# Matmuls of 64 rows alternating between the partition halves in a two-layer attention and expert kernel, with the copies and waits around them moved

## The chip, the cores and the metric

The kernel runs on one core of a Trainium2 chip. The metric is the device time of one execution, in microseconds (us). All times are of the same program with the same inputs.

## The reference

256 tokens of width 1024 go through two layers. Each layer has a mixing part and an expert part:

```python
c_q, c_kv, k_r, n_q, n_kv, n_gate, m_gate = jnp.split(x @ w_in, offsets, axis=-1)
y_mla = mla_attention(q_nope, q_rope, k_nope, k_rope, v) @ w_branch_mla
y_nsa = nsa_attention(qn, kc, vc, k_sel, ..., k_win, ..., nsa_gates) @ w_branch_nsa
mixed = (g_mla * y_mla + g_nsa * y_nsa) @ w_out
x = layer_norm(DEEPNORM_ALPHA * x + mixed, ln1_g, ln1_b)
x = layer_norm(DEEPNORM_ALPHA * x + peer(x, ...), ln2_g, ln2_b)
```

`mla_attention` has eight heads with keys of 96 values (64 plus 32 rotary). `nsa_attention` has eight heads with keys of 64 values in two groups, and three branches: compressed keys (15 per group), selected blocks and a window; with 256 tokens the last two see every earlier token. `peer` scores 128 keys in each of two halves for eight heads (`s = einsum('thpd,hpnd->thpn', q, sub_keys)`, 64 values a half), takes the best 16 of each half and the best 16 of their 256 sums, and adds up those experts out of 128 x 128:

```python
a = jnp.einsum('chkd,cd->chk', expert_u[ec], xc)
w = gc * jax.nn.gelu(a, approximate=False)
y = jnp.einsum('chk,chkd->cd', w, expert_v[ec])
```

## The kernel before, in words

Weights come in tiles of 128 x 1024 through a ring of four slots (`raw`). SyncE loads a tile once TensorE has let go of its slot. ScalarE rounds it to `hi` (`split_hi`, L457), VectorE subtracts to get `lo` (`split_lo`, L710), and TensorE multiplies lo by hi, hi by lo and hi by hi (L1208 to L1210, 24 passes a tile; L1219 in the other orientation). A split runs three tiles ahead of its use (`AHEAD`). Every engine's order is written out by hand. An engine takes its instructions in that order, and semaphores say when a piece of data may be read (`acc_ready`, `tr_ready`, `wide_ready`) or a PSUM bank overwritten (`acc_read`, `tr_read`). `acc` and `tr` are two PSUM banks each, `wide` four.

A layer runs like this. The front part has 68 weight tiles: projections, then the transposes of queries and keys (`transpose_heads`, L1315), four on one bank of `tr` at a time; ScalarE copies bank 0 away and VectorE bank 1. The blocks for the compressed keys are multiplied by `w1` (L1347), then by `w2` (L1354), and the scores against the 15 compressed keys are eight matmuls for each of two token tiles (L1365). The attention has 12 units of four heads: `mla`, `sel` or `win`, six for each token tile, with 128 keys in the first six and 256 in the rest. For unit u TensorE makes the scores (`scores`, L1376: two heads in each of two banks, then a matmul that adds the mask, L1396), one gate tile, the transposes of unit u - 1 and the outputs of the unit before. VectorE takes the maximum (L958), ScalarE the exponentials (L585), and VectorE scales them (L971, `p_ready`), copies, splits a tile (L997) and goes on to the next unit. In `sel` and `win` the operands `nqT` and `nkT` have 64 rows, and all lie in partitions 0 to 63.

The expert part first projects the queries (`pqT`). The key scores are four rounds (L1501): in a round four matmuls with rows 0 to 63 go to bank 0 of `acc`, then four with rows 64 to 127 to bank 1; ScalarE copies both to `scr` (L634), and the next round needs the bank free. Then 128 tiles of `peer_u` follow, in 16 turns of 8 (`u_tile`). Beside them VectorE chooses the experts: `route(i)` (L1055) has 14 stages for one head of one token tile, 16 such units in all. `route(0)` runs ahead of the loop, and turn i of the loop runs `route(i + 1)` with the eight splits of tiles 8i + 3 to 8i + 10 spread through its stages (L1098). After the last one come `best_ready` (L1116) and `places_b` (`whole_ready`, L1117). TensorE waits for `places_b` at L1531, ahead of the last turn of `u_tile`, and inside that turn for `best_ready` after e = 1 and for `picks_ready` after e = 2. ScalarE follows each tile with a Gelu (L641) and the next split. Then the gates are built from one-hot matrices (L1551), and 128 tiles of `peer_v` follow.

## Time and profile before

| | |
|---|---|
| median of three runs | 2342.13 us (2337.15 to 2342.89) |
| the profiled execution | 2342.61 us |
| its span, first to last instruction | 2341.0 us |
| mean granted clock of TensorE | 0.966 |
| TensorE busy | 2202.3 us, 94% of the span |
| VectorE, ScalarE, GpSimd busy | 64%, 50%, 7% |

A row of a timeline gives the start, the busy time in us, the engine, the line, the operation with what it writes and reads, and how many instructions the row merges; in brackets stands the idle time of the engine just before it and what ended it. PE is TensorE's matmul, PEld its loading of weights, which overlaps matmuls; DVE is VectorE and ACT is ScalarE. An fp32 matmul shows as two passes, so four matmuls are x8. [...]

### The profile page before, as it was taken

To read this page: it belongs to the slowest core of one execution; us is meant where nothing else is said; L and a number is where in the kernel's file an instruction comes from. 1 tells how busy PE (TensorE), PEld (TensorE's weight loads), DVE (VectorE), ACT (ScalarE), POOL (GpSimd) and SP (SyncE) were. 2 spreads that over 40 slices of the span, in tenths; PEclk is the share of its full clock that TensorE was granted. 3 is DMA by queue.
4 is the path that set the end of the run, shared out by engine and by line. 5 is a ranking of instruction groups with operands and counts; after the bars stand their busy time and mean duration, and the time that the engine had idled before them with its cause. 6 is when DMAs were issued, how large, how long until landed. Compare 5 with 4: busy or idle time off the path is not lost.

```text
span 2341.0 us, 42801 instructions
## 1 busy us (share of the span) xinstructions
PE 2202.3 (94%) x14216; PEld 1976.2 (84%) x14216; DVE 1504.8 (64%) x2768; ACT 1166.1 (50%) x1836; POOL 164.0 (7%) x176
## 2 busy tenths in 40 slices
PE   6989979999999999999979899899999999999997
PEld 5887779999998788788777877899999977887886
DVE  5546557777776955555557465677777678555555
ACT  4335444545546845445434354454554477544553
POOL 1000000000004700000000000000000065000000
PEclk9979989999999999999979799999999999999999
DMA  4622335555552055555536114355555411555554
GB/s 146 214 73 83 118 117 171 183 184 179 182 176 73 0 188 190 198 194 192 172 129 229 55 64 141 122 184 182 180 184 182 162 45 37 196 197 190 195 190 142
DMA packets 96310, 353.49 MB, mean 151 GB/s; under 512 B 11056, under 2 KB 11088, under 8 KB 95856
## 3 DMA queue, kind: packets, MB, share of 16 engines
q1 hardware_dynamic: 94032, 341.90, 44.5%
q0 software_dynamic: 2208, 10.66, 1.3%
q8 instruction: 43, 0.70, 0.1%
q14 instruction: 27, 0.22, 0.0%
HBM read 351.47 MB, written 1.05 MB: 151 GB/s over the span
## 4 chain that ended last, share of the span: by engine, by line
PE 63%; issue 27%; ACT 3%; DVE 3%; POOL 2%; DMA 2%; POOLq 0%; ACTq 0%; SPq 0%; DVEq 0%
PE wide L1219 13%; PE acc L1208 13%; PE acc L1209 13%; PE acc L1210 13%; PE acc L1551 3%; POOL hot_i L443 2%; DMA raw<-in_front 1%; ACT hot_i L669 1%; PE wide L1394 1%; PE acc L1347 1%; PE tr L1319 1%; ACT hi L457 1%; POOL rstd L412 0%; PE acc L1442 0%; PE acc L1365 0%
## 5 line engine op out<-in xcount | busy, mean ns | idle before, releaser
L710 DVE TENSOR_TENSOR lo<-raw,hi 128x1024 fp32r<-128x1024 f32 x648 | 792.3, 1224 | 607.0 <-ACT hi L457 601.5
L457 ACT ACTIVATE hi<-raw 128x1024 fp32r<-128x1024 f32 x648 | 686.7, 1060 | 535.8 <-DMA raw<-in_peer_v 353.1
L1208 PE MATMUL acc<-xT_hi,lo 128*128 128x256 f32 x2560 | 736.4, 288 | 18.3 <-DVE places_b L1117 9.0
L1209 PE MATMUL acc<-xT_lo,hi 128*128 128x256 f32 x2560 | 733.2, 286 | 0.0
L1210 PE MATMUL acc<-xT_hi,hi 128*128 128x256 f32 x2560 | 732.9, 286 | 0.0
L1208 PEld LDWEIGHTS acc<-xT_hi,lo 128*128 128x128 f32 x2560 | 501.0, 196 | 22.4 <-issue 20.4
L1209 PEld LDWEIGHTS acc<-xT_lo,hi 128*128 128x128 f32 x2560 | 500.9, 196 | 0.1
L1210 PEld LDWEIGHTS acc<-xT_hi,hi 128*128 128x128 f32 x2560 | 500.5, 196 | 0.0
L1219 PE MATMUL wide<-hi,w_lo 128*128 128x512 f32 x1024 | 317.2, 391 | 11.9 <-DVE w_lo L1165 11.9
L1219 PE MATMUL wide<-hi,w_hi 128*128 128x512 f32 x1024 | 316.7, 391 | 0.0
L1219 PE MATMUL wide<-lo,w_hi 128*128 128x512 f32 x1024 | 316.3, 390 | 0.0
L641 ACT ACTIVATE big<-acc 128x256 f32 (+1 forms) x256 | 98.5, 385 | 339.2 <-PE acc L1210 339.2
L1219 PEld LDWEIGHTS wide<-hi,w_lo 128*128 128x128 f32 x1024 | 192.6, 189 | 54.5 <-DVE lo L710 10.8
L1219 PEld LDWEIGHTS wide<-lo,w_hi 128*128 128x128 f32 x1024 | 192.8, 188 | 40.4
L1219 PEld LDWEIGHTS wide<-hi,w_hi 128*128 128x128 f32 x1024 | 192.9, 188 | 40.2
L443 POOL TENSOR_TENSOR hot_i<-iota,picksT 128x512 f32<-128x512 f32 x128 | 133.1, 1041 | 869.6 <-PE acc L1210 838.3
L1551 PEld LDWEIGHTS acc<-hot_j,hot_i 128*128 128x128 f32 x1024 | 128.9, 196 | 38.3 <-ACT hot_i L669 28.6
L1551 PE MATMUL acc<-hot_j,hot_i 128*128 128x128 f32 x1024 | 146.1, 287 | 10.9 <-ACT hot_i L669 8.8
L1165 DVE TENSOR_TENSOR w_lo<-big,w_hi 128x256 fp32r<-128x256 f32 x256 | 106.8, 418 | 1.1 <-ACT w_hi L689 1.1
L689 ACT ACTIVATE w_hi<-big 128x256 fp32r (+1 forms) x256 | 102.2, 400 | 2.8 <-DVE big L1148 2.8
L1148 DVE TENSOR_TENSOR big<-acc,big 128x512 f32 (+1 forms) x128 | 87.6, 684 | 15.4 <-PE acc L1551 14.5
L669 ACT ACTIVATE hot_i<-hot_i,ones 128x512 f32<-128x512 f32 x128 | 90.3, 707 | 0.0
(243 smaller groups left out, 1873.4 us busy)
## 6 DMA issues: line engine op xcount, KB each, us to landing
raw<-in_peer_u SPq DMA_DIRECT2D x256, 512.0 KB, 3.3
raw<-in_peer_v SPq DMA_DIRECT2D x256, 512.0 KB, 3.3
raw<-in_front SPq DMA_DIRECT2D x136, 512.0 KB, 3.4
ln_par<-in_ln POOLq DMA_DIRECT2D x10, 512.0 KB, 5.1
w<-in_cmp_w POOLq DMA_DIRECT2D x2, 2048.0 KB, 8.8
xs<-in_x SPq DMA_DIRECT2D x2, 512.0 KB, 7.0
keys<-in_sub_keys POOLq DMA_DIRECT2D x2, 512.0 KB, 3.6
out<-xs SPq DMA_DIRECT2D x1, 1024.0 KB, 3.9
```

The source lines that it names most:

```text
L443: nc.gpsimd.tensor_tensor(hot_i[:, e], iota[:].unsqueeze(1).broadcast_to([P, 4, P]), toks, ALU.subtract).then_inc(differences_ready, 1)
L457: nc.scalar.activation(hi[:, s], raw[:, s], ACT.Identity).then_inc(hi_done, 1)
L641: nc.scalar.activation(big[:, i * 2 + e // JB, :, e % JB], acc[:, e % 2, :SEQ].rearrange("p (g t) -> p g t", t=TB), ACT.Gelu).then_inc(acc ...
L669: nc.scalar.activation(hot_i[:, e], hot_i[:, e], ACT.Relu, bias=ones[:, 0:1], scale=-1.0).then_inc(hot_i_ready, 1)
L689: nc.scalar.activation(w_hi[:, s].rearrange("p (g t) -> p g t", t=TB), big[:, i + c // JB, :, c % JB], ACT.Identity).then_inc(w_hi_done, 1)
L710: nc.vector.tensor_tensor(lo[:, s], raw[:, s], hi[:, s].bitcast(F32), ALU.subtract).then_inc(lo_done, 1)
L1165: nc.vector.tensor_tensor(w_lo[:, s].rearrange("p (g t) -> p g t", t=TB), big[:, i + c // JB, :, c % JB], part, ALU.subtract).then_inc(w_l ...
L1208: mm(dst, lo[:, s, c], xh[:, k], start=k == 0, stop=False)
L1209: mm(dst, hi[:, s, c], xl[:, k], start=False, stop=False)
L1210: ins = mm(dst, hi[:, s, c], xh[:, k], start=False, stop=k == DK - 1)
L1219: ins = mm(wide[:, tt, 512 * h:512 * h + width], a[:, tok], w[:, s, off:off + width], start=first and k == 0, stop=last and k == 2)
L1551: ins = mm(acc[:, e % 2, r * P:(r + 1) * P], hot_i[:, e, r], hot_j[:, e, r], start=True, stop=True)
```

## The change

Queries and keys of `nsa_attention` now fill both partition halves. `nqT` holds head 2j in rows 0 to 63 and head 2j + 1 in rows 64 to 127, and takes four transposes a token tile instead of eight. `nkT` holds each key twice, once in each half: two new copies on VectorE (`nk_tok`) write them side by side for the transpose. The compressed scores, the `sel` and `win` scores and the expert key scores issue matmuls in turn from the one half and the other, each half with its own bank, and the two masks of a unit come after its four matmuls. VectorE copies bank 1 of the key scores. `kc` is made twice, once for each half. On VectorE the split of `peer_u`'s tile 3 moves into `route(0)`, turn i of the loop splits tiles 8i + 4 to 8i + 11, and `route(0)` waits for all the key scores. In the last turn the waits for `best_ready` and `picks_ready` move one tile later, and that for `places_b` from ahead of the turn to after e = 4.

```diff
@@ scores of the compressed keys, TensorE
-                    for h in range(HEADS):
-                        g = h // 4
-                        ins = mm(acc[:, (A_CS + tt) % 2, h * 16:h * 16 + NCMP], nqT[:, h, tt * P:(tt + 1) * P],
-                                 kc[:, g * NCMP:(g + 1) * NCMP], start=True, stop=True)
-                    ins.then_inc(acc_ready, 1)
+                for i in range(HEADS):
+                    tt, pair = divmod(i, 4)
+                    for par in range(2):
+
+                        g, half = pair // 2, slice(par * HD, par * HD + HD)
+                        ins = mm(acc[:, par, i * 16:i * 16 + NCMP], nqT[half, pair, tt * P:(tt + 1) * P],
+                                 kc[half, g * NCMP:(g + 1) * NCMP], start=True, stop=True)
...
@@ scores of sel and win, TensorE
+                        for h in range(2):
+                            for b in range(2):
+                                half = slice(b * HD, b * HD + HD)
+                                mm(banks[:, b, h, :keys_n], nqT[half, 2 * hg + h, tok],
+                                   nkT[half, (0 if kind == "sel" else GROUPS) + hg, :keys_n],
+                                   start=h == 0, stop=False, skip_group_check=True)
+                        for b in range(2):
+                            ins = masked(b)
...
@@ rotary part, VectorE
+                    nc.vector.tensor_copy(nk_tok[:, tt], rot[:, tt, HEADS + GROUPS:].unsqueeze(2).broadcast_to([P, 4, 2, HD]))
...
@@ transposes, TensorE
-                for g in range(4):
-                    tt, hg = divmod(g, 2)
-                    transpose_heads(X_NQ + g, [rot[:, tt, 4 * hg + j] for j in range(4)], HD)
...
+                for tt in range(TT):
+                    transpose_heads(X_NQ + tt, [rot[:, tt, 2 * j:2 * j + 2].rearrange("p a d -> p (a d)") for j in range(4)], P)
...
@@ key scores, VectorE
+                for c in range(4):
+                    dve.wait_ge(acc_ready, l * NREADY + R_SCR + 2 * c + 2)
+                    nc.vector.tensor_copy(scr[:, 4 * c:4 * c + 4, P:], acc[:, 1].rearrange("p (u n) -> p u n", u=4)
+                                          ).then_inc(acc_read[1], 1)
                 for b in range(2):
-                    dve.wait_ge(acc_read[b], OPEN + l * (NACC // 2) + A_SCR // 2 + 1)
+                    dve.wait_ge(acc_read[b], OPEN + l * (NACC // 2) + A_U // 2)
...
@@ choice of the experts, VectorE
-                        for e in range(8):
-                            if turn is not None and split_after[e] == g:
+                        for e in splits:
+                            if split_after[e - splits[0]] == g:
                                 after_route(turn, e)
...
-                route(0)
-                for b in range(2):
-                    dve.wait_ge(acc_read[b], OPEN + l * (NACC // 2) + A_U // 2)
-                dve.sem_inc(apart, 1)
+                route(0, 0, range(1))
                 with dve.Fori(0, NKEYS // 8 - 1) as i:
-                    route(i + 1, i)
+                    route(i + 1, i, range(1, 9))
...
@@ last turn, TensorE
-                pe_.wait_ge(whole_ready, 4 + l + 1)
-                wide_free(l, W_V)
                 for e in range(8):
                     u_tile(NKEYS // 8 - 1, e)
-                    if e == 1:
+                    if e == 2:
                         pe_.wait_ge(best_ready, l + 1)
...
-                    if e == 2:
+                    if e == 3:
                         pe_.wait_ge(picks_ready, l + 1)
...
-                    if e == 3:
+                    if e == 4:
+                        pe_.wait_ge(whole_ready, 4 + l + 1)
+                        wide_free(l, W_V)
```

Three places show how instructions stand now. The first is VectorE between the query projection and the second stage of `route(0)`, before:

```order
L710 TENSOR_TENSOR lo<-raw,hi 128x1024 [waits hi_done]
L1046 REGISTER_ALU
L1046 COMPARE_AND_BRANCH
L1051 REGISTER_ALU
L1066 COPY r_s<-scr 128x256 [waits acc_read0,acc_read1]
L157 ISA
L1067 MAX r_v<-r_s 128x8 [waits route_step]
L1067 MAX r_v<-r_s 128x8
L157 REGISTER_ALU
L1068 MATCH_REPLACE r_s_110<-r_v,r_s 128x128 [waits route_step]
```

and with the change (L713 is the split, L1057 the copy of key scores):

```order
L713 TENSOR_TENSOR lo<-raw,hi 128x1024 [waits hi_done]
L1051 REGISTER_ALU
L1051 COMPARE_AND_BRANCH
L1056 REGISTER_ALU
L1057 COPY scr<-acc 128x4x128 [waits acc_ready]
...
L1060 REGISTER_ALU
L1075 COPY r_s<-scr 128x256 [waits acc_read0,acc_read1]
L162 ISA
L1076 MAX r_v<-r_s 128x8 [waits route_step]
L1076 MAX r_v<-r_s 128x8
L712 REGISTER_ALU
L713 TENSOR_TENSOR lo<-raw,hi 128x1024 [waits hi_done]
```

Four copies now stand ahead of `route(0)`, and a split (tile 3) stands inside it; the next split, tile 4, comes after the second stage of `route(1)`.

The second is TensorE in a `sel` unit of the first token tile, before and with the change:

```order
L1394 MATMUL wide<-nkT,nqT 128x128 [waits exp_ready]
L1394 MATMUL wide<-nkT,nqT 128x128
L1396 MATMUL wide<-causal_r,ident_r 128x2x128
L1394 MATMUL wide<-nkT,nqT 128x128 x2
L1396 MATMUL wide<-causal_r,ident_r 128x2x128
```

```order
L1411 MATMUL wide<-nkT,nqT 128x128 [waits exp_ready]
L1411 MATMUL wide<-nkT,nqT 128x128 x3
L1397 MATMUL wide<-causal_r,ident_r 128x2x128 x2
```

The four matmuls of 64 rows now stand together ahead of both masks.

The third is TensorE in the last turn of `u_tile`, at the one-hot matmuls that read `places_b`, with the change:

```order
L1216 MATMUL acc<-xT_hi,hi 128x256
L1560 REGISTER_ALU
L1207 REGISTER_ALU [waits whole_ready]
L1540 MATMUL wide<-next_b,places_b 128x512 [waits wide_read1,wide_read0]
L1543 MATMUL wide<-minus_iota,ones_b 128x512
```

The wait for `whole_ready` now stands right ahead of its first reader; before it stood ahead of the turn's first tile.

## Rows read from the trace of the kernel before

**Rows 1.** Page, part 1: busy us (share of the span) and instructions by engine.
```profile
PE 2202.3 (94%) x14216; PEld 1976.2 (84%) x14216; DVE 1504.8 (64%) x2768; ACT 1166.1 (50%) x1836; POOL 164.0 (7%) x176
```
**Rows 2.** Waits of TensorE: total us, times, longest.
```profile
PE acc L1208 <- DVE places_b L1117: 9.0, 2, 4.5
```
**Rows 3.** Timeline of VectorE at the transposes of the first layer.
```profile
131.44 2.35 DVE L710 TENSOR_TENSOR lo<-raw,hi 128x1024 fp32r<-128x1024 f32 x2
134.09 0.68 DVE L899 TENSOR_SCALAR nqT<-tr 64x512 f32<-64x512 f32 x1 [0.30 <-PE tr L1319]
135.56 0.68 DVE L899 TENSOR_SCALAR nqT<-tr 64x512 f32<-64x512 f32 x1 [0.78 <-PE tr L1319]
```
**Rows 4.** Compressed scores: TensorE's timeline, then L1365 in two stretches (us, busy, clock).
```profile
163.00 5.26 PE L1365 MATMUL acc<-kc,nqT 64*128 64x15 f32 x32 [0.59 <-DVE vc L922]
...
163.00:164.90 1.90, 1.90 (x17) 1.90 (x18) 1.00 0.88 276
164.90:168.20 3.30, 3.30 (x17) 3.25 (x16) 0.51 0.00 0
```
**Rows 5.** Timeline of TensorE: outputs of an mla unit.
```profile
191.25 0.66 PE L1437 MATMUL acc<-pT,v_mla 128*64 128x128 f32 x8
```
**Rows 6.** Timeline of TensorE: scores of an mla unit, then of a sel unit.
```profile
180.36 0.61 PE L1394 MATMUL wide<-kT,qT 96*128 96x128 f32 x4
...
180.93 0.61 PE L1394 MATMUL wide<-kT,qT 96*128 96x128 f32 x4
...
186.03 0.71 PE L1394 MATMUL wide<-nkT,nqT 64*128 64x128 f32 x4
...
186.99 0.71 PE L1394 MATMUL wide<-nkT,nqT 64*128 64x128 f32 x4
```
**Rows 7.** Timeline of VectorE in the attention of the first layer.
```profile
210.92 1.23 DVE L710 TENSOR_TENSOR lo<-raw,hi 128x1024 fp32r<-128x1024 f32 x1 [1.16 <-ACT hi L457]
...
219.55 1.23 DVE L958 TENSOR_REDUCE negmax<-wide 128x4 f32<-128x1024 f32 x1 [0.85 <-PE wide L1396]
...
226.62 1.23 DVE L958 TENSOR_REDUCE negmax<-wide 128x4 f32<-128x1024 f32 x1 [0.42 <-PE wide L1396]
...
234.15 1.22 DVE L958 TENSOR_REDUCE negmax<-wide 128x4 f32<-128x1024 f32 x1 [0.68 <-PE wide L1396]
```
**Rows 8.** Timeline at the key scores of the first layer.
```profile
343.09 1.52 PEld L1507 LDWEIGHTS acc<-keys,pqT 64*128 64x128 f32 x16 [0.79 <-issue]
...
344.23 1.23 DVE L710 TENSOR_TENSOR lo<-raw,hi 128x1024 fp32r<-128x1024 f32 x1 [1.56 <-ACT hi L457]
344.28 1.15 ACT L634 ACTIVATE scr<-acc 128x512 f32<-128x512 f32 x2
344.93 1.52 PEld L1507 LDWEIGHTS acc<-keys,pqT 64*128 64x128 f32 x16 [0.32 <-ACT scr L634]
```
**Rows 9.** Timeline at the start of the peer_u tiles.
```profile
345.57 0.29 DVE L1066 COPY r_s<-scr 128x256 f32<-128x256 f32 x1
...
346.64 0.09 DVE L1068 MATCH_VALUE_LOAD r_s<-r_v,r_s 128x8 f32 x1
...
350.62 0.38 PE L1208 MATMUL acc<-xT_hi,lo 128*128 128x256 f32 x1 [0.29 <-ACT scr L634]
...
354.16 1.05 ACT L457 ACTIVATE hi<-raw 128x1024 fp32r<-128x1024 f32 x1
...
357.21 1.21 DVE L710 TENSOR_TENSOR lo<-raw,hi 128x1024 fp32r<-128x1024 f32 x1
```
**Rows 10.** The wait before the last turn, and two stretches (PE, PEld, DVE, ACT, POOL, clock).
```profile
700.97 0.58 PE L1208 MATMUL acc<-xT_hi,lo 128*128 128x256 f32 x1 [4.51 <-DVE places_b L1117]
...
700.80:704.30 3.50, 3.33 (x15) 3.33 (x16) 0.00 (x0) 0.00 (x0) 0.00 (x0) 0.51 0.02 5
350.60:364.00 13.40, 13.38 (x111) 13.39 (x112) 11.38 (x38) 5.36 (x9) 0.00 (x0) 1.00 0.40 126
```

More of the change, by code:

```diff
@@ L130, in unit, with place_of @@
     return kind, hg, tt, tt * 4 + O_OF[i], tr
+def place_of(u, h):
+    return h if unit(u)[0] == "mla" else 2 * (h % 2) + h // 2
 class Steps:
@@ L204, in build @@
         sq = at("sq", [P, 8, SEQ], F32, 104 * K)
+        nk_tok = at("nk_tok", [P, TT, 4, 2, HD], F32, 104 * K)
         sc = at("sc", [P, 2, 4, SEQ], F32, 104 * K)
@@ L542, in _ @@
                         heads_copy(first + g, dst[:QKD, 4 * hg:4 * hg + 4, tt * P:(tt + 1) * P], QKD, g % 2)
-                for g in range(0, 4, 2):
-                    tt, hg = divmod(g, 2)
-                    heads_copy(X_NQ + g, nqT[:, 4 * hg:4 * hg + 4, tt * P:(tt + 1) * P], HD, 0, NSA_SCALE)
-                heads_copy(X_KT, nkT[:, :, 0:P], HD, 0)
+                heads_copy(X_NQ, nqT[:, :, 0:P], P, 0, NSA_SCALE)
+                heads_copy(X_KT, nkT[:, :, 0:P], P, 0)
                 heads_copy(X_CD, cmpT[:, :, 0:P], P, 0)
@@ L653, in _ @@
                     gelu_tile(NKEYS // 8 - 1, e)
[L654 removed]
+                    if e == 1:
                         act.wait_ge(best_ready, l + 1)
@@ L1048, in _, with route @@
                         split_lo(l, (i + (T_PQ + e + AHEAD) // SLOTS), (T_PQ + e + AHEAD) % SLOTS)
+                for c in range(4):
+                    dve.wait_ge(acc_ready, l * NREADY + R_SCR + 2 * c + 2)
+                    nc.vector.tensor_copy(scr[:, 4 * c:4 * c + 4, P:], acc[:, 1].rearrange("p (u n) -> p u n", u=4)
+                                          ).then_inc(acc_read[1], 1)
                 for b in range(2):
-                    dve.wait_ge(acc_read[b], OPEN + l * (NACC // 2) + A_SCR // 2 + 1)
+                    dve.wait_ge(acc_read[b], OPEN + l * (NACC // 2) + A_U // 2)
                 dve.sem_inc(apart, 1)
-                def route(i, turn=None):
+                def route(i, turn, splits):
                     rt = Steps(dve, route_step, (l * 16 + i) * ROUTE_STEPS, ROUTE_STEPS, apart)
@@ L1124, in _ @@
                                         ALU.mult).then_inc(picks_ready, 1)
+                after_route(NKEYS // 8 - 1, 1)
                 tr_copy(l, X_PK, picksT[:, 0:2], tr[:, X_PK % 2].rearrange("p (k t) -> p k t", k=2))
-                after_route(NKEYS // 8 - 1, 1)
+                after_route(NKEYS // 8 - 1, 2)
                 tr_copy(l, X_PK + 1, picksT[:, 2], tr[:, (X_PK + 1) % 2, :SEQ])
-                for e in range(2, 7):
+                for e in range(3, 7):
                     after_route(NKEYS // 8 - 1, e)
@@ L1329, in _ @@
                 pe_.wait_ge(tok_ready, l * TT + TT)
-                for g in range(4):
-                    tt, hg = divmod(g, 2)
-                    transpose_heads(X_NQ + g, [rot[:, tt, 4 * hg + j] for j in range(4)], HD)
                 for tt in range(TT):
-                    transpose_heads(X_KT + tt, [rot[:, tt, HEADS + GROUPS + j] for j in range(4)], HD)
+                    transpose_heads(X_NQ + tt, [rot[:, tt, 2 * j:2 * j + 2].rearrange("p a d -> p (a d)") for j in range(4)], P)
+                for tt in range(TT):
+                    transpose_heads(X_KT + tt, [nk_tok[:, tt, j].rearrange("p a d -> p (a d)") for j in range(4)], P)
                 for tt in range(TT):
@@ L1353, in _ @@
                 b = A_KCVC % 2
-                mm(acc[:HD, b, 0:nb], w2[:, 0], hid[:, 0], start=True, stop=True)
+                for half in range(2):
+                    mm(acc[half * HD:(half + 1) * HD, b, 0:nb], w2[:, 0], hid[:, 0], start=True, stop=True)
                 for g in range(GROUPS):
@@ L1503, in _ @@
                         acc_free(l, A_SCR + 2 * c + p)
-                        rows = slice(p * HD, (p + 1) * HD)
-                        for r in range(4):
+                    for r in range(4):
+                        for p in range(2):
+                            rows = slice(p * HD, (p + 1) * HD)
                             tt, h = divmod(4 * c + r, HEADS)
```

77 lines of the change are left out of this document (38 added, 39 removed).

## The prediction

> **What bounds the kernel now.** I read the page first, then the waits of TensorE, then stretches of the timeline where the diff acts. TensorE is busy for 94% of the span and VectorE for 64% [rows 1]. So an edit pays only where TensorE does less on its own account, or where it waits. Its waits on the places that the diff touches are few: the list gives 9.0 us in two waits for places_b, 4.5 us in each layer [rows 2]. The diff acts at six places in each of two layers. The two layers read alike, so I work out one and double it.
>
> **Transposes (L1330 to L1338).** The eight transposes of the queries of a token tile become four, so one pair of groups (bank 0, bank 1) goes. VectorE takes its copies of bank 1 1.47 us apart (134.09 to 135.56) [rows 3], and that is the pace of the pairs. Against that, VectorE gets two copies of 128x512 (nk_tok) ahead of tok_ready. No row has that copy from SBUF. A half as wide one takes 0.29 us [rows 9], and one of that width out of PSUM 0.68 us [rows 3]. Bounds are therefore 0.3 and 0.7 each, and I take 0.48, near the first because both ends of it lie in SBUF. The two splits behind them then end 0.96 us later than 133.79, which is 0.66 us past the moment when VectorE takes its first copy now. Net: 1.47 - 0.66 = **0.8 us saved** (0.1 to 1.4).
>
> **Compressed scores (L1365).** 32 passes (two for each fp32 matmul) take 163.00 to 168.2, that is 5.2 us. 17 of them fit in 1.90 us at the granted clock 1.00 (0.11 us each), the others need 0.2 us at 0.51 [rows 4]. All read the same 64 rows, so each waits for the one ahead. Do alternating halves run side by side? Two rows say yes. The outputs of L1437, which alternate the output half, put 8 passes in 0.66 us: less 0.27 for the last, 0.056 us each [rows 5]. And in the key scores 16 weight loads of two row halves fit in 1.52 us, where 0.11 each would make 1.8 us [rows 8]. 32 passes at 0.056 are 1.8 us, or about 3.4 at the low clock. I take 2.0: **3.2 us saved** (0 to 3.4). The doubled matmul for kc costs 0.1 us.
>
> **Attention scores (L1394).** For "mla" (96 rows) two matmuls and a mask take 0.57 us (180.36 to 180.93). For "sel" and "win" (64 rows) they take 0.96 us (186.03 to 186.99) [rows 6]. The passes have the same width, so the 0.39 us is what it costs to go from 64 rows to 128 and back. The change goes there and back once in a unit instead of twice and runs the two halves together, so TensorE loses some 0.8 us less per unit (0.39 for the change of rows, some 0.45 for matmuls that overlap). That is 6.4 us in eight units, more where 256 keys are scored. But the loop through VectorE (maximum, then ScalarE's exponentials, then scaling) is nearly as long as TensorE's. VectorE waits for the scores only 0.85, 0.42 and 0.68 us, and once 1.16 us for a split whose ScalarE waited for TensorE [rows 7]. Once these are gone the loop is VectorE's own. I take the three in full and 0.65 of the fourth: **2.6 us saved** (1.3 to 3.1). The other 4 us turn into waits of TensorE for p_ready.
>
> **Key scores (L1507).** In each of the four rounds ScalarE copies both banks, 1.15 us, and TensorE starts the next round at 344.93 [rows 8]. Now VectorE copies bank 1. But VectorE has a split in front of that copy: it starts at 344.23 and holds the engine to about 345.4. A copy of 0.68 us [rows 3] then ends at 346.1, and as TensorE waits for both banks, round two begins 1.15 us later than now. The later rounds are tied to one bank: passes 0.85, last pass 0.27, copy 0.68 (VectorE) against 0.58 (ScalarE), handing over 0.1. That is 1.9 us against 1.84 now, and the shorter last round gives back about what the longer rounds cost. Net **1.2 us lost** (0.1 saved to 1.5 lost). [...]
>
> **Start of the experts' first pass (L1528, tiles of peer_u).** Now VectorE runs route(0) from 345.57, beside the key scores, and splits tile 3 at 357.21. TensorE starts tile 0 at 350.62; a tile is 24 passes of 0.12 us, 2.88 us [rows 9, 10]. The change delays route(0) until all eight banks are copied, which is about when tile 0 starts, and puts tile 3's split after its second stage. That split waits for hi, which ends 4.59 us after tile 0 began (354.16 + 1.05 - 350.62). It takes 1.15 us, so VectorE goes on at 5.8 us. It must then run the rest of route(0) and the first two stages of route(1) before it splits tile 4. That piece is in the trace of before without any split or long wait: 346.64 to 357.21, 10.57 us [rows 9]. Tile 4's split starts at 16.4 and ends at 17.6 us; TensorE wants it at 4 x 2.88 = 11.5 us. **A new wait of 6.1 us.** Later splits come every 2.2 to 2.7 us and keep ahead. What does such a wait do to the clock? After the 4.51 us wait at 700.97 the granted clock was 0.51 in the next 3.5 us, with some 16 passes of 0.21 us instead of 29 [rows 10], so about 1.5 us of work lost. I take the same here (0 to 3.0): **7.6 us lost**.
>
> **End of that pass (L1531).** TensorE waits for places_b before tile 120. VectorE makes it after it has split tile 122, about one and a half tiles later [rows 2, 10]. The change asks for it after tile 124 and for best_ready after tile 122. With VectorE one tile ahead, best_ready comes about 4 us after tile 120 ends, while TensorE wants it 5.8 us after, so 1.7 us of cover are left. ScalarE's wait for best_ready (under 1 us, before tile 124's hi) has tile 124's split behind it, done some 4.3 us after tile 121; it is wanted at 5.8. So the 4.5 us go, and the 1.5 us of low clock after them: **6.0 us saved** (0 to 6.0).
>
> **The sum.** Per layer: -0.8 - 3.2 + 0.1 - 2.6 + 1.2 + 7.6 - 6.0 = -3.7 us. Twice that is -7.4. The profiled execution took 2342.61 us, 0.5 over the median of 2342.13. So **2335.2 us**, 6.9 us or 0.30% under the median. That is just on the line of 0.3% (7.0 us), which is about what a measurement of this kernel can tell from no change.
>
> **Rivals.**
> A. *Front ahead of the clock.* Shorter thin stretches in front of the gate tiles also leave less low clock. For: 3.3 of the 5.2 us of L1365 ran at 0.51 and so did the tile after it. Against: low stretches of fixed length may fall anywhere. 1.5 us more per layer at two places: -6, 2329 us. Chance 0.19.
> B. *The first tiles are hidden.* VectorE reaches tile 4 in time. Nothing in the rows speaks for it beyond my chance of a slip in reading the order. The 15.2 us are not lost: 2320 us. Chance 0.06.
> C. *Two copiers.* [...] Chance 0.04.
> D. *Halves take turns.* Alternating gives no overlap and only the changes of rows are saved: nothing at the compressed scores (+3.2), half at the attention (+1.3). +9 in all: 2344 us. Against: rows 5 and 8. Chance 0.12.
> E. *More low clock.* The new wait, or the thinner key scores before it, bring 6.8 us of low clock instead of 3.4; or best_ready is late and 1 us of wait stays. Some 3 us per layer: 2341 us. Chance 0.12.
> F. *Slower: each change of half drains the array.* If going from one half to the other costs 0.2 us, half of what a group pays for there and back [rows 6], then the compressed scores have 15 such changes (+3.0, and +3.2 not saved), the key scores 31 (+6.2) and the attention units 3 each (+1.6 beyond what VectorE hides, and the 2.6 not saved). Per layer 16.6 over my sum: 2368 us. It ends slower from about 0.05 us a change. Against: in rows 8 two halves follow each other without a gap. Chance 0.07. [...]
>
> **Chances and range.** My forecast has 0.40, split evenly by the line of 0.3%. Faster: 0.20 + 0.19 + 0.06 + 0.04 = 0.49, less 0.01 for A falling short: 0.48. Same: 0.20 of the forecast, most of D and E (0.21): 0.41. Slower: F and what is left of D and E, 0.11. Range: downward to A and C with their own spread and short of B, upward to D: 2324 to 2345 us; B and F are outside.
>
> **What would show it.** Right: 32 passes of compressed scores in about 2 us; 0.3 us or less of waits of VectorE for the scores, and TensorE waiting for the scaled sc instead; the first VectorE copy of the key scores behind a split; a TensorE wait of about 6 us for lo some 11.5 us after tile 0 of peer_u, twice, with low clock behind it; no wait for places_b. Wrong: tile 4 without a wait (B), passes still 0.11 us apart in L1365's place (D), gaps at each change of half (F), or a wait of 4 us at best_ready.

## The result and the profile after

The changed kernel took 2343.97 us (median of 20 runs, 2338.87 to 2350.34), beside 2340.6 us for the kernel before on the same chip. The ratio is 1.0017 with a 95% interval of 1.0009 to 1.0025: 0.17%, some 4 us, slower. That lies within the 0.3% that was called no change, and within the range of 2324 to 2345 us, but the forecast was 2335.2 us, 0.30% faster. One of the 20 executions of the kernel before took 8244 us, where the other 19 took 2334.66 to 2344.42; it is no part of the ratio. The profiled execution took 2343.9 us (2342.61 before), its span is 2341.5 us and the mean granted clock of TensorE 0.964 (0.966). Granted clocks are shares of the full clock, which reads 1.00.

The engines' busy times, from part 1 of the page; TensorE has 19.5 us less work than in [rows 1], in the same span:

```profile
PE 2182.8 (93%) x14204; PEld 1960.9 (84%) x14204; DVE 1510.4 (65%) x2782; ACT 1159.4 (50%) x1826; POOL 163.8 (7%) x176
```

The waits of TensorE at the places of the change (total us, times, longest). The one for places_b [rows 2] is gone. New are one for the split of tile 4 (the first line) and one for the copied key scores (the second). The one for the split of the attention's output (the third) has grown from 1.1 us in two waits to 5.5 in four:

```profile
PE acc L1214 <- DVE lo L713: 11.2, 2, 5.6
...
PE acc L1526 <- DVE scr L1057: 7.3, 6, 1.9
...
PE acc L1214 <- DVE oT_lo L990: 5.5, 4, 1.8
```

The timeline of the changed kernel at the steps in front of the attention and in it: VectorE's new copy and its copies out of `tr`, then TensorE's compressed scores, then the scores of a `sel` unit with the two masks.

```profile
128.98 0.43 DVE L894 COPY nk_tok<-rot 128x512 f32<-128x512 f32 x1
...
131.80 0.68 DVE L901 TENSOR_SCALAR nqT<-tr 128x512 f32<-128x512 f32 x1
133.29 0.69 DVE L723 COPY nkT<-tr 128x512 f32<-128x512 f32 x1 [0.81 <-PE tr L1325]
...
159.36 1.96 PE L1374 MATMUL acc<-kc,nqT 64*128 64x15 f32 x32 [0.69 <-DVE vc L923]
...
178.23 0.72 PE L1411 MATMUL wide<-nkT,nqT 64*128 64x128 f32 x8
178.88 0.50 PE L1397 MATMUL wide<-causal_r,ident_r 128*128 128x256 f32 x2
```

The 32 passes of the compressed scores take 1.96 us instead of 5.26 [rows 4]. Four `sel` matmuls of 64 rows start and make way for the mask within 0.65 us (178.23 to 178.88), where two took 0.71 [rows 6]. So matmuls of the two halves do run side by side.

The key scores, on all three engines:

```profile
335.54 1.16 PE L1526 MATMUL acc<-keys,pqT 64*128 64x128 f32 x16 [0.67 <-ACT pqT L632]
...
336.63 1.22 DVE L713 TENSOR_TENSOR lo<-raw,hi 128x1024 fp32r<-128x1024 f32 x1 [1.61 <-ACT hi L463]
336.70 0.60 ACT L638 ACTIVATE scr<-acc 128x512 f32<-128x512 f32 x1
337.78 0.68 DVE L1057 COPY scr<-acc 128x512 f32<-128x512 f32 x1
...
338.61 2.08 PE L1526 MATMUL acc<-keys,pqT 64*128 64x128 f32 x16 [1.91 <-DVE scr L1057]
340.69 0.60 ACT L638 ACTIVATE scr<-acc 128x512 f32<-128x512 f32 x1 [3.39 <-PE acc L1526]
340.73 0.69 DVE L1057 COPY scr<-acc 128x512 f32<-128x512 f32 x1 [2.27 <-PE acc L1526]
...
341.57 2.08 PE L1526 MATMUL acc<-keys,pqT 64*128 64x128 f32 x16 [0.89 <-DVE scr L1057]
```

A first round of 1.16 us, then a stand of 1.91 us behind VectorE's split and copy, as forecast: round two starts 3.07 us after round one, where it was 1.81. But then 16 passes take 2.08 us, not 1.16: the granted clock has fallen to 0.50, after TensorE had stood for 0.67 us, worked for 1.16 and stood again. Both banks become full at one moment, so that neither copy runs beside matmuls. The next answer is of two stretches; its columns are the bounds, us, busy time of PE, PEld, DVE, ACT and POOL, the granted clock (third from the right), DMA share and GB/s. They are the last three key-score rounds, then tile 0 of `peer_u` (4.71 us) and the start of tile 1.

```profile
338.60:347.40 8.80, 6.23 (x48) 5.41 (x48) 2.07 (x3) 1.79 (x3) 0.00 (x0) 0.50 0.01 2
347.40:352.60 5.20, 5.18 (x28) 5.19 (x29) 0.78 (x3) 0.18 (x1) 0.00 (x0) 0.62 0.00 0
```

And the kernel before, all four rounds and then the first 7 us of tiles (2.97 us for tile 0), at the full clock throughout:

```profile
343.10:350.60 7.50, 6.81 (x64) 6.06 (x64) 5.38 (x23) 5.31 (x9) 0.00 (x0) 1.00 0.21 73
350.60:357.60 7.00, 6.98 (x58) 6.99 (x59) 5.27 (x17) 2.41 (x5) 0.00 (x0) 1.00 0.24 75
```

The stage from the first key score to tile 0 of `peer_u` grew from 7.50 us in both layers to 11.88 and 10.76. The forecast wait at tile 4 is there:

```profile
353.78 1.23 DVE L713 TENSOR_TENSOR lo<-raw,hi 128x1024 fp32r<-128x1024 f32 x1 [5.37 <-ACT hi L463]
...
365.27 1.21 DVE L713 TENSOR_TENSOR lo<-raw,hi 128x1024 fp32r<-128x1024 f32 x1
...
366.54 0.58 PE L1214 MATMUL acc<-xT_hi,lo 128*128 128x256 f32 x1 [5.61 <-DVE lo L713]
```

Tile 0 started at 347.42, and TensorE stands from 360.93 to 366.54 in front of tile 4.

The attention took 76.18 us in each layer, against 75.48 and 75.07, though TensorE has less to do in it. Its two stretches, before and then with the change; the clock stands at 0.96 and 0.97, and then at 0.89:

```profile
180.36:255.84 75.48, 71.21 (x498) 56.17 (x496) 44.12 (x105) 37.15 (x128) 0.00 (x0) 0.96 0.17 57
1336.90:1411.97 75.07, 70.83 (x498) 55.67 (x496) 44.13 (x105) 37.15 (x128) 0.00 (x0) 0.97 0.17 57
```
```profile
172.56:248.74 76.18, 68.25 (x497) 54.53 (x496) 44.31 (x105) 37.13 (x128) 0.00 (x0) 0.89 0.18 56
1333.11:1409.29 76.18, 68.26 (x497) 54.53 (x496) 44.30 (x105) 37.13 (x128) 0.00 (x0) 0.89 0.17 56
```

VectorE in the attention of the first layer, to be read beside [rows 7]: its wait for the split, and its two waits for scores of 256 keys:

```profile
202.37 1.23 DVE L713 TENSOR_TENSOR lo<-raw,hi 128x1024 fp32r<-128x1024 f32 x1 [0.42 <-ACT hi L463]
...
212.47 1.22 DVE L963 TENSOR_REDUCE negmax<-wide 128x4 f32<-128x1024 f32 x1 [1.18 <-PE wide L1397]
...
237.76 1.23 DVE L963 TENSOR_REDUCE negmax<-wide 128x4 f32<-128x1024 f32 x1 [0.89 <-PE wide L1397]
```

### The profile page after: what moved, and what is told of

It reads as the page before. It is cut to its first block, busy times and chain, and to the rows that moved or that the text cites. A ratio compares the mean times of both kernels' runs of the same rounds, so it can differ in the third digit from the quotient of the medians.

```text
span 2341.5 us, 42777 instructions
## 1 busy us (share of the span) xinstructions
PE 2182.8 (93%) x14204; PEld 1960.9 (84%) x14204; DVE 1510.4 (65%) x2782; ACT 1159.4 (50%) x1826; POOL 163.8 (7%) x176
## 4 chain that ended last, share of the span: by engine, by line
PE 58%; issue 28%; DVE 5%; ACT 4%; POOL 2%; DMA 2%; POOLq 0%; ACTq 0%; DVEq 0%; SPq 0%
PE wide L1225 14%; PE acc L1214 12%; PE acc L1215 12%; PE acc L1216 12%; PE acc L1571 3%; POOL hot_i L449 2%; DMA raw<-in_front 1%; ACT hot_i L672 1%; PE acc L1352 1%; ACT sc L590 1%; DVE lo L713 1%; ACT hi L463 1%; PE tr L1325 1%; DVE negmax L963 1%; PE acc L1460 1%
## 5 line engine op out<-in xcount | busy, mean ns | idle before, releaser
L713 DVE TENSOR_TENSOR lo<-raw,hi 128x1024 fp32r<-128x1024 f32 x648 | 792.4, 1224 | 594.2 <-ACT hi L463 589.6
```

Of the source, the lines that this page charges most:

```text
L713: nc.vector.tensor_tensor(lo[:, s], raw[:, s], hi[:, s].bitcast(F32), ALU.subtract).then_inc(lo_done, 1)
```

## The experiments

All kernels were run beside the kernel before, and ratios are to it. 0.1% is 2.3 us. "The halves" are the changed operands, transposes, compressed scores and unit scores. The first three runs put parts of the change into the kernel before; the fourth leaves out the new key scores alone.

### The halves alone

```diff
@@ the changed kernel, with key scores, splits and the wait for places_b put back
-                for c in range(4):
-                    dve.wait_ge(acc_ready, l * NREADY + R_SCR + 2 * c + 2)
...
-                route(0, 0, range(1))
+                route(0, 0, range(0))
-                    route(i + 1, i, range(1, 9))
+                    route(i + 1, i, range(8))
```

> The kernel before with the halves alone: doubled keys, four transposes instead of eight, compressed scores and the scores of sel and win in two row halves, the order with the masks last. Key scores, splits and the wait for places_b stay as before. Theory 1 (the halves save time of TensorE, and thinner work pays part of it back in low clock): up to the routing this is the changed kernel, so transposes to w1 about 9.5 us, compressed scores 2.6 us, gate 6 to compressed softmax 7.3 us, attention 76 us; that is -1.0 -2.4 -1.8 +0.9 = -4.3 us in a layer, key scores 7.5 us as before, wait for places_b 4.5 us still there: about 2333 us, 0.35% under before. Theory 2 (VectorE's loop through the attention takes all that TensorE saves, and the small stages move only into waits): within 2 us of before.

2326.99 us, ratio 0.9947 (0.9932 to 0.9961): 12.4 us faster, 6.2 in a layer. That is more than the 4.3 us a layer that theory 1 drew from the changed kernel's stages, and leaves no room for theory 2. The halves are a gain. The interval leaves 4.6 to 8.0 us a layer.

### The late wait for places_b alone

```diff
@@ the kernel before, last turn, TensorE
-                pe_.wait_ge(whole_ready, 4 + l + 1)
-                wide_free(l, W_V)
                 for e in range(8):
                     u_tile(NKEYS // 8 - 1, e)
...
                     if e == 3:
+                        pe_.wait_ge(whole_ready, 4 + l + 1)
+                        wide_free(l, W_V)
```

> The kernel before with TensorE's wait for places_b alone moved from before tile 120 to after tile 123, ahead of its first reader. Theory 1 (the wait and the low clock behind it are lost time): the 4.5 us wait goes in each layer, up to 1.5 us of low clock with it, 9 to 12 us in all, 2329 to 2332 us. Theory 2 (the wait was cover for something later, best_ready or the split of tile 124): a wait of 2 to 4 us appears at best_ready after tile 121 or at lo of tile 124, and the time falls by less than 4 us.

2324.34 us, ratio 0.9939 (0.9925 to 0.9953): 14.3 us faster, a little more than the 9 to 12 of theory 1. Nothing took the wait's place. From the first `peer_u` tile to the last, TensorE is now busy for every microsecond, at the full clock (stretch of this kernel, columns as above):

```profile
345.98:717.89 371.91, 371.91 (x3086) 370.06 (x3086) 274.01 (x657) 185.88 (x258) 0.00 (x0) 1.00 0.54 179
```

That pass took 378.1 us before, 6.2 more: 4.5 of wait and 1.7 of low clock.

### Halves and late wait together

The first experiment's kernel, with the late wait put in:

```diff
@@ last turn, TensorE
-                pe_.wait_ge(whole_ready, 4 + l + 1)
-                wide_free(l, W_V)
                 for e in range(8):
                     u_tile(NKEYS // 8 - 1, e)
...
                     if e == 3:
+                        pe_.wait_ge(whole_ready, 4 + l + 1)
+                        wide_free(l, W_V)
```

> Halves and the late wait for places_b together, key scores and splits as before. Theory 1: the two add up, -4.3 and -5 to -6 us in a layer, 2320 to 2324 us; that would show that the alternating key scores with VectorE's copies and the splits moved by one tile cost the changed kernel some 20 us. Theory 2 (they overlap, or low clock elsewhere takes them): 2330 us or more.

2312.14 us, ratio 0.9894 (0.9875 to 0.9913). The two add up, to more than theory 1 gave. So this part of the change is worth some 25 us, and the rest of the change costs all of that and 4 us more. I call this kernel the best one below; its second run, told last, gave 0.9886, and 0.9890 is the mean of both.

### The changed kernel with the old key scores

```diff
@@ the changed kernel, ScalarE and TensorE at the key scores
+                for i in range(8):
+                    c, p = divmod(i, 2)
+                    act.wait_ge(acc_ready, l * NREADY + R_SCR + i + 1)
...
                     for p in range(2):
                         acc_free(l, A_SCR + 2 * c + p)
-                    for r in range(4):
-                        for p in range(2):
-                            rows = slice(p * HD, (p + 1) * HD)
+                        rows = slice(p * HD, (p + 1) * HD)
+                        for r in range(4):
```

> The changed kernel with key scores as before: one bank after the other, ScalarE copies both, VectorE none. The splits stay one stage later. Theory 1 (the new wait at tile 4 of peer_u comes of the order of splits and routing on VectorE, not of its four copies): key scores back to 7.5 us from 11.9 and 10.8, the wait for lo at tile 4 stays at 5.6 us (5 to 6.5), since route(0) and tile 0 move together: some 3.3 to 4.4 us less in a layer, 2335 to 2337 us. Theory 2 (the copies push VectorE behind, and without them the wait goes too): the wait at tile 4 under 3 us and 2328 us or less.

2327.76 us, ratio 0.9958 (0.9944 to 0.9973). The wait at tile 4 stayed as theory 1 said, and so theory 2 falls, though the time is the one that it gave:

```profile
PE acc L1215 <- DVE lo L715: 11.7, 2, 5.9
```

But the time fell by 13.8 us (1.0017 to 0.9958), about twice what the stage's own 4.4 and 3.3 us explain. Most of the rest is right behind it: tile 0 no longer runs at the lower clock (1.00 now in the first layer, where it was 0.58) and takes 2.97 us in both layers instead of 4.71 and 5.03. Against the best kernel (0.9890) the moved splits cost 0.68%, 15.9 us or 8.0 in a layer.

### Which part of the key scores: four runs

New key scores on the best kernel, splits as before; against the changed kernel:

```diff
-                route(0, 0, range(1))
+                route(0, 0, range(0))
...
-                    route(i + 1, i, range(1, 9))
+                    route(i + 1, i, range(8))
```

> The halves and the late wait, with the changed kernel's key scores (alternating halves, VectorE copies bank 1) and the splits where they were before. Beside the kernel with halves and late wait alone (ratio 0.9894, 2312 us) it differs in the key scores and in when route(0) begins. Theory 1 (the key scores are thin, the clock falls over them and over the first tiles of peer_u, and the delayed routing makes VectorE late for tile 3): key scores 10.5 to 12 us instead of 7.5, a wait of 3 to 5 us for lo at tile 3 or 4, 6 to 9 us lost in a layer: 2324 to 2330 us. Theory 2 (only the wait at tile 4 was dear, and it comes of the splits moved by a stage): no such wait, 1.2 us lost in a layer: 2314 us.

2332.4 us, ratio 0.9968 (0.9955 to 0.9981), so 18 us lost against 0.9890, the upper end of the 6 to 9 us a layer of theory 1. The key scores took 8.89 us in the first layer, where the clock held (1.00), and 11.74 in the second, where it fell (0.50 over the last three rounds); TensorE waited 2.7 and 2.4 us for the split of tile 3, less than the 3 to 5 of theory 1. The first layer shows the new key scores at the full clock (TensorE's timeline of this kernel):

```profile
334.44 1.16 PE L1526 MATMUL acc<-keys,pqT 64*128 64x128 f32 x16 [0.67 <-ACT pqT L632]
337.27 1.16 PE L1526 MATMUL acc<-keys,pqT 64*128 64x128 f32 x16 [1.67 <-DVE scr L1057]
339.31 1.16 PE L1526 MATMUL acc<-keys,pqT 64*128 64x128 f32 x16 [0.88 <-DVE scr L1057]
```

A later round takes 2.04 us there, against 1.84 before and 1.9 forecast, and the stage 1.4 us more than before, against 1.2 forecast. The clock fell only as tile 0 began, which took 4.47 us at 0.62.

The changed kernel with TensorE bank by bank:

```diff
                     for p in range(2):
                         acc_free(l, A_SCR + 2 * c + p)
-                    for r in range(4):
-                        for p in range(2):
-                            rows = slice(p * HD, (p + 1) * HD)
+                        rows = slice(p * HD, (p + 1) * HD)
+                        for r in range(4):
```

> The changed kernel with TensorE's key scores bank by bank again (four matmuls of half 0 into bank 0, then four of half 1 into bank 1), ScalarE copying bank 0 and VectorE bank 1 as in the change. Theory 1 (what costs is the wait for the slower of two copies after thin work; alternating makes each round's matmuls shorter and ends both banks at the same moment, so that nothing overlaps with the copies): bank 0 ends early and its copy runs beside bank 1's matmuls, rounds of 1.9 to 2.2 us, the stage 9 us or less, 2 to 3 us less in a layer than in the changed kernel, 2337 to 2340 us. Theory 2 (VectorE's place behind its split sets the rounds, whatever the order on TensorE): rounds of 2.9 us and 2344 us as in the changed kernel.

2330.39 us, ratio 0.9971 (0.9958 to 0.9983): 10.8 us less than the changed kernel, twice what theory 1 gave. VectorE's copies are as in the change. The last rounds shrank from 2.96 to 1.94 us, the stage to 8.17 and 7.73, and the clock held at 1.00. The timeline of this kernel between the second round and the third (a row of 16 passes is bank 1 of the one and bank 0 of the next): TensorE stands for 0.22 us only, since one bank is copied while the other fills.

```profile
338.17 1.71 PE L1525 MATMUL acc<-keys,pqT 64*128 64x128 f32 x16 [0.22 <-DVE scr L1057]
339.36 0.69 DVE L1057 COPY scr<-acc 128x512 f32<-128x512 f32 x1 [1.25 <-PE acc L1525]
339.92 0.60 ACT L638 ACTIVATE scr<-acc 128x512 f32<-128x512 f32 x1 [1.33 <-PE acc L1525]
340.11 1.71 PE L1525 MATMUL acc<-keys,pqT 64*128 64x128 f32 x16 [0.23 <-DVE scr L1057]
```

The changed kernel with ScalarE copying both banks:

```diff
-                for c in range(4):
-                    dve.wait_ge(acc_ready, l * NREADY + R_SCR + 2 * c + 2)
-                    nc.vector.tensor_copy(scr[:, 4 * c:4 * c + 4, P:], acc[:, 1].rearrange("p (u n) -> p u n", u=4)
-                                          ).then_inc(acc_read[1], 1)
...
```

> The changed kernel with ScalarE copying both banks of the key scores; alternating order on TensorE, and route(0) still behind the last copy. Theory 1 (alternating order itself opens the stage: both banks become full together, so TensorE stands for both copies, 1.15 us, in every round, and the clock falls): rounds of 2.1 us at the full clock, or 3.1 us where it is low, the stage 8.5 to 12 us. Theory 2 (VectorE's split ahead of its copy is the cost): the stage 7.5 to 8.5 us, and as in the kernel with the old key scores 2328 us.

2342.92 us, ratio 1.0012 (1.0001 to 1.0024): not to be told from the change, with VectorE's copies out of it. The stage took 11.89 us in both layers. Its rounds, of this kernel's timeline, are 3.3 us: 2.08 of matmuls at a clock of 0.50, 1.23 of standing.

```profile
335.41 2.08 PE L1524 MATMUL acc<-keys,pqT 64*128 64x128 f32 x16 [1.23 <-ACT scr L639]
337.48 1.08 ACT L639 ACTIVATE scr<-acc 128x512 f32<-128x512 f32 x2 [2.22 <-PE acc L1524]
...
338.71 2.08 PE L1524 MATMUL acc<-keys,pqT 64*128 64x128 f32 x16 [1.23 <-ACT scr L639]
```

The changed kernel with matmuls whose result nobody reads behind each round:

```diff
+                wide_free(l, W_V)
...
                             if r == 3:
                                 ins.then_inc(acc_ready, 1)
+                    for _ in range(7):
+                        mm(wide[:, 0, :256], ident_r[:], causal_r[:].unsqueeze(1).broadcast_to([P, 2, P]), start=True, stop=True)
```

> The changed kernel with seven more matmuls of 128 rows and 256 columns on TensorE behind each round of key scores, into a buffer that nobody reads: they add no dependence and fill the time in which TensorE stands for the copies. Theory 1 (TensorE's standing lets the granted clock fall, and the low clock over key scores and first tiles is what costs): the clock stays at 1.00 there, rounds of 2.0 us or less behind the first, tile 0 of peer_u 2.9 us instead of 5, the stage 9 us or less in spite of the added work, 2 to 5 us less in a layer, 2334 to 2340 us. Theory 2 (the copies set the rounds, the clock does not matter): the stage stays at 10.8 to 12 us or grows by the added work of up to 0.8 us in the last round, 2344 to 2346 us.

2333.94 us, ratio 0.9978 (0.9968 to 0.9989): 9.1 us **less** than the changed kernel, with 28 matmuls more in each layer. The filler and the key scores of this kernel, and two stretches, the rounds and the first tiles:

```profile
337.83 1.10 PE L1532 MATMUL wide<-causal_r,ident_r 128*128 128x256 f32 x7
...
338.86 1.16 PE L1527 MATMUL acc<-keys,pqT 64*128 64x128 f32 x16
```
```profile
336.70:343.00 6.30, 6.26 (x69) 5.65 (x70) 2.07 (x3) 1.80 (x3) 0.00 (x0) 1.00 0.01 3
343.00:350.00 7.00, 7.00 (x60) 7.00 (x59) 3.06 (x12) 2.12 (x4) 0.00 (x0) 1.00 0.21 78
```

The clock is 1.00 where it was 0.50 and 0.62, a round takes 2.12 us instead of 2.96 and the stage 8.99 and 9.00. This parts the cost of the new key scores in the profiles: 1.5 us is order, copies and split together (7.5 to 9.0, at the full clock), 2.9 and 1.8 us are low clock in the stage, and 1.8 and 2.1 us low clock in tile 0 (2.94 us here).

### VectorE's copies alone, on the best kernel

TensorE and splits as in the best kernel; ScalarE copies bank 0 and VectorE bank 1, and `route(0)` comes after its copies:

```diff
@@ the best kernel, VectorE ahead of route(0)
+                for c in range(4):
+                    dve.wait_ge(acc_ready, l * NREADY + R_SCR + 2 * c + 2)
+                    nc.vector.tensor_copy(scr[:, 4 * c:4 * c + 4, P:], acc[:, 1].rearrange("p (u n) -> p u n", u=4)
+                                          ).then_inc(acc_read[1], 1)
                 for b in range(2):
-                    dve.wait_ge(acc_read[b], OPEN + l * (NACC // 2) + A_SCR // 2 + 1)
+                    dve.wait_ge(acc_read[b], OPEN + l * (NACC // 2) + A_U // 2)
```

> Halves and late wait (ratio 0.9894) plus, of the new key scores, only that VectorE copies bank 1, with route(0) behind its four copies; TensorE goes bank by bank and the splits stand where they were before. Theory 1 (two copiers do not shorten the stage, since TensorE never needed more than one, and VectorE's delayed routing then makes tile 3 of peer_u late): key scores 7.7 to 8.2 us instead of 7.5, a wait of 2 to 4 us for lo at tile 3, 3 to 5 us lost in a layer, 2318 to 2322 us, ratio 0.992 to 0.994. Theory 2 (two copiers help, and only the alternating order was bad): key scores 7 us or less and 2312 us or less.

2328.15 us, ratio 0.9953 (0.9937 to 0.9969). Theory 1 was right in kind: key scores 7.98 and 7.78 us, no gain from the second copier. But the loss against the best kernel is 14.7 us, where it gave 6 to 10, and the wait at tile 3 is 5.1 us in both layers, where it gave 2 to 4. The timeline of this kernel shows why:

```profile
343.54 0.29 DVE L1075 COPY r_s<-scr 128x256 f32<-128x256 f32 x1
...
355.32 1.21 DVE L713 TENSOR_TENSOR lo<-raw,hi 128x1024 fp32r<-128x1024 f32 x1
...
356.58 0.58 PE L1214 MATMUL acc<-xT_hi,lo 128*128 128x256 f32 x1 [5.10 <-DVE lo L713]
```

`route(0)` starts 0.94 us after tile 0 (342.60). In the best kernel it starts 5.05 us ahead of it (336.31 against 341.36), and its tile 3 is split at 349.16, 0.84 us before it is wanted (341.36 + 3 x 2.88):

```profile
336.31 0.29 DVE L1073 COPY r_s<-scr 128x256 f32<-128x256 f32 x1 [0.31 <-ACT scr L639]
...
347.95 1.21 DVE L715 TENSOR_TENSOR lo<-raw,hi 128x1024 fp32r<-128x1024 f32 x1
```

5.05 + 0.94 - 0.84 = 5.15 us late; the wait is 5.10. So the late `route(0)` by itself makes the same wait as the moved splits by themselves (5.9), and together they make it once (5.6).

### The attention: two runs on the best kernel

The 64-row score matmuls twice over:

```diff
                         for h in range(2):
                             for b in range(2):
                                 half = slice(b * HD, b * HD + HD)
                                 mm(banks[:, b, h, :keys_n], nqT[half, 2 * hg + h, tok],
...
+                        for h in range(2):
+                            for b in range(2):
+                                half = slice(b * HD, b * HD + HD)
+                                mm(banks[:, b, h, :keys_n], nqT[half, 2 * hg + h, tok],
...
```

> Halves and late wait (2312 us in its own runs) with the 64-row score matmuls of sel and win issued twice, the second time over the first: 16 more passes pairs of two halves, that is 0.2 to 0.5 us more work of TensorE per unit, 2 to 4 us in a layer's attention, and nothing else. Theory 1 (the halves leave TensorE with less work in the attention, the granted clock falls there and takes the gain): the mean granted clock of the attention rises from 0.93 to 0.95 or more, its 74.0 us do not grow and may fall to 73, total 2308 to 2313 us. Theory 2 (the clock falls for other reasons; the loop through VectorE sets the pace): clock as it is, attention 74 to 76 us, total 2312 to 2317 us.

2317.56 us, ratio 0.9909 (0.989 to 0.9929). With twice the matmuls the attention did not grow: 73.80 and 73.02 us, against 74.08 and 73.95. The clock went from 0.93 to 0.97 and 0.98. The same unit near the end shows it, TensorE of the best kernel, and then of this one (the second issue of the scores is a row of its own, 1.03 us, not shown):

```profile
229.98 1.75 PE L1326 MATMUL tr<-ident,sc 128*128 128x128 f32 x8 [1.75 <-DVE sc L978]
...
234.61 2.08 PE L1412 MATMUL wide<-nkT,nqT 64*128 64x256 f32 x8
```
```profile
229.48 1.14 PE L1326 MATMUL tr<-ident,sc 128*128 128x128 f32 x8 [0.80 <-DVE sc L978]
...
232.14 1.14 PE L1412 MATMUL wide<-nkT,nqT 64*128 64x256 f32 x8
```

In the best kernel TensorE waits longer for `sc` (1.75 us instead of 0.80); then the clock is down (0.50 instead of 1.00) and the same matmuls take 2.08 us instead of 1.14. As to the attention theory 1 holds, but the total lies above its 2308 to 2313 us. In the whole time no gain is seen: the interval overlaps that of the best kernel, and its six runs spread from 2310.9 to 2324.3 us.

Bank by bank with the masks between:

```diff
-                        for h in range(2):
-                            for b in range(2):
+                        for b in range(2):
+                            for h in range(2):
...
-                        for b in range(2):
                             ins = masked(b)
```

> Halves and late wait with the score matmuls of sel and win in the order of before: one bank's two matmuls, now both of one row half, its mask, then the other bank's. No two neighbours of different halves, and the change between 64 and 128 rows twice in a unit again. Theory 1 (the alternating order saves TensorE 0.8 us in a unit, but the loop and the clock keep most of it): the first four matmuls and two masks of a unit take 1.9 us instead of 1.3, the attention 73.5 to 75 us at a higher clock, total 2311 to 2315 us. Theory 2 (the order matters in full): attention 2 us or more longer, 2316 us or more.

2315.51 us, ratio 0.9892 (0.9877 to 0.9907), the same as the best kernel. The attention took 75.02 and 75.67 us, and its clock is back at 0.97 and 0.96. The alternating order of the unit scores is thus worth nothing in the whole time that these runs can tell.

### The best kernel again

> Halves and late wait once more, with nothing else changed, beside the kernel before on this chip: if its first figure holds, ratio 0.988 to 0.991, 2311 to 2317 us.

2313.43 us, ratio 0.9886 (0.9867 to 0.9905). It is faster than both the kernel before and the changed one. Its profiled execution took 2321.9 us, and shows one thing more: the clock fell in the key scores of the second layer though their code is as before (columns as above).

```profile
1482.98:1492.70 9.72, 9.59 (x64) 9.17 (x64) 7.18 (x31) 5.19 (x8) 0.00 (x0) 0.63 0.18 56
```

In the profiles of all kernels whose TensorE goes bank by bank there it fell in 1 of 20 such stages; in those with alternating order and no filler in 5 of 6, and in the sixth 0.1 us behind it.

## Why the prediction was wrong, point by point

Measured in runs, per layer, each part added to the ones before: the halves -6.2 us (forecast -0.8 - 3.2 + 0.1 - 2.6 = -6.5); the late wait -6.7 (forecast -6.0); the moved splits +8.0 (forecast +7.6); the new key scores +6.9 (**forecast +1.2**). The sum is +2.0, the forecast -3.7, and the difference of 5.7 us is that one term. Each ratio is known to about 0.15%, so each of these figures to 2 or 2.5 us. The last two depend on their order: without the moved splits the new key scores cost 9.1 us, since their late `route(0)` then makes a wait of its own.

- **Transposes, -0.8.** Right. From the first transpose of `rot` to `w1` the profile shows -1.3 and -0.8 us. The new copy took 0.43 us, the estimate was 0.48.
- **Compressed scores, -3.2.** Right: 1.96 us, forecast 2.0. That row excludes rival D (halves take turns) and F (each change of half drains): a pass costs 0.055 us, where [rows 5] gave 0.056. The 0.1 us for the doubled matmul of `kc` was my estimate, with no row for it: its two passes (0.30 us) became four in 0.31.
- **Attention, -2.6.** Wrong in the changed kernel's profile: +0.7 and +1.1. Of VectorE's waits in [rows 7] those of 0.42 and 0.68 us went and the one for the split shrank from 1.16 to 0.42. But the one of 0.85 grew to 1.18, and one of 0.89 is new; the sign asked for 0.3 or less. And the step "the other 4 us turn into waits of TensorE" took such waits as free. They are not. Among them the clock fell, to a mean of 0.89 from 0.96 and 0.97, one period from maximum to maximum grew from 7.15 to 8.63 us and the last from 5.28 to 6.25; three others shrank, to 5.43, 6.56 and 6.87 us from 6.18, 7.07 and 7.53. The best kernel's attention took 74.1 and 74.0 us, but the old one took 74.4 and 74.5 in the kernel with the late wait alone, so that no gain of the attention by itself is shown. What can be told is the stretch from the first compressed score to the attention's last outputs: 92.8 and 92.4 us before and 93.1 and 93.3 with the late wait alone, against 89.4 in both layers of the changed kernel and 90.0 and 89.8 in the best one. That is some 3.3 us saved, where these two steps were forecast at 5.7. The halves as a whole came out as forecast in the runs all the same; the transposes bring some 1 us of it, and the rest lies in untouched stages, which in these profiles differ by up to 2 us each with where the clock was low, and I cannot place it.
- **Key scores, +1.2.** This step failed, and by one thing: it priced no low clock. Its working for the full clock was right. It had the matmuls and the copy of a round one behind the other, 1.9 us, and the second round 1.15 us late behind VectorE's split. Where the clock held at 1.00, the rounds took 2.04 us, the second came 1.02 us late, and the stage cost 1.4 us; with the filler, with which the clock stayed at 1.00, 1.5. But the same sum leaves TensorE standing for some 0.8 us in each round, and nothing was put down for that, though the prediction put 1.5 us behind the wait at tile 4. TensorE stood for 0.9 to 1.9 us a round, and got the lower clock in the stage (0.50) and in tile 0 of `peer_u` (0.58 in the first layer); a filler gave back 4.6 of the 6.9 us. The alternating order is what opens these stands: with it the term is 5.4 us a layer larger than bank by bank (1.0017 against 0.9971), while VectorE's copies bank by bank cost 1.5 (0.9971 against 0.9958), no more than these ratios can tell from nothing. Rival E named this place and called it 3 us a layer, with a chance of 0.12; it was the one that happened, nearly twice as large.
- **Rival C.** No run shows a gain from a second copier, to which the prediction gave a chance of 0.04 and which stands in its chance of faster and in its range: 7.98 and 7.78 us against 7.50 on the kernel with the old order. ScalarE's copy of one bank, 0.60 us, had been hidden behind the matmuls into the other, and VectorE was wanted elsewhere.
- **Start of the pass, +7.6.** Right in place, count and size: 5.61 us forecast as 6.1, at tile 4, twice, with 1.4 to 2.4 us of low clock behind it in the kernels that have it at tile 4 (forecast 1.5). Tile 4's split began 17.85 us after tile 0 (forecast 16.4), since hi of tile 3 waits for a tile 0 that was slow; TensorE was 2.0 us later for the same reason. Not seen was that the late `route(0)` alone is enough for such a wait.
- **End of the pass, -6.0.** Right: 6.2 us in the pass, nothing in its place.
- **Rival B** falls with the row at 366.54. **Rival A** was seen at one place only: from the first compressed score to the softmax's transposes it took 9.87 us instead of 14.03 and 14.07, 1 us more than the sum had, but the attention lost it again. The best kernel, with the same code there, shows the exchange: that stretch took 12.6 us in both layers and the attention 2.1 and 2.2 us less than in the changed kernel.

## What to carry to other kernels

Before matmuls into two banks are interleaved to run side by side, see what the copies out of those banks overlap with: filling both at once made the matmuls of a round 0.55 us shorter (1.16 us instead of 1.71), yet the round no shorter at the full clock (2.04 us against 1.94) and 1 us longer at the 0.50 that its waits brought (2.96). Where an edit turns work of TensorE into waits of TensorE, read the granted clock of the next stretch and price it; here the new key scores cost 1.5 us a layer at the full clock and the low clock 4.6 more. And split a large change into its parts even when the sum is near zero: here two parts brought 26 us and two took 30.

## What the runs showed of the hardware

- More work held the clock up, twice, and once made the kernel faster: 28 matmuls a layer that nobody reads, beside the key scores, took 9.1 us off the kernel, with the granted clock at 1.00 instead of 0.50; doubled score matmuls left the attention no longer and its clock 0.04 and 0.05 higher, with no gain in the whole time.
- Alternating 64-row matmuls of the two halves start every 0.055 us at the full clock (32 in 1.96 us, with the last one's own time), all in one half every 0.11 [rows 4].
- Low stretches of 3.4 us and of twice that were seen: in the attention of the changed kernel the clock was 0.50 from 204.60 to 208.00 and from 231.90 to 238.70 us, 1.00 between them. The prediction counted with such lengths.
- Where the low stretches fall differs between executions of one kernel: the key scores of the second layer took 7.50 us at 1.00 in one profiled execution of the best kernel and 9.72 at 0.63 in the other. It differs between kernels with the same attention code too, which took 76.2 us in both layers of the changed kernel (0.89) and 74.6 and 72.2 in those of the kernel with the old key scores (0.91 and 0.95). A stage's time from one profile is good to some 2 us here; the verdicts above rest on the ratios of runs.
